# HGRN and retention rounds of a hybrid decoder layer: another order on ScalarE and DVE, and two groups of small matmuls in 64-column tiles

## The chip, the cores and the metric

The kernel runs on one core of a Trainium2 chip. The metric is the device time of one launch in microseconds (us). The kernel before takes 937.84 us, the median of 3 runs (936.68 to 938.04). TensorE, whose matmuls are called PE below, multiplies; ScalarE (ACT) and DVE read its sums from PSUM; GpSimd (POOL) works in SBUF alone; SyncE (SP) issues the weight loads.

## The reference, cut to what matters

One layer for 512 prompt rows and 8 sample rows (TT = 520 columns in the kernel, which holds everything transposed):

```
xn = rmsnorm(h); u = xn @ w_in      # hq hf hi hg (HGRN), rq rk rv rg (retention), ga gb
HGRN, 8 heads of 64:  f = lb + (1-lb)*sigmoid(hf);  S_t = diag(f_t) S_{t-1} + (1-f_t) i_t^T
                      o_t = S_t^T silu(hq_t)        # chunk by chunk for the prompt, one step for samples
retention, 4 heads of 128:  R_t = gamma R_{t-1} + k_t v_t^T,  o_t = R_t^T q_t   (rotary q, k)
a = head_rmsnorm(o) * g * silu(gate)                # for each branch
h += (sigmoid(ga)*(a_hg @ w_br_hg) + sigmoid(gb)*(a_r @ w_br_ret)) @ w_out
h += (gelu(causal_conv3(up_a)) * up_g) @ w_down;  h += sigmoid(rmsnorm(h) @ w_ple_gate) * (p @ w_ple)
y = rmsnorm(h)
```

Everything is float32.

## The kernel before

Every product with a weight matrix is done in units of 128 output rows. A unit needs `whi`, the weight rounded to the fast matmul format (made by ACT from the loaded `raw`, L832), and `wlo = raw - whi` (made by DVE, L1169, the "weight subtraction"). It is then 3 matmul pairs for each 128 rows of the inner dimension (hi by hi, hi by lo, lo by hi), 48 matmuls of 260 columns for the usual 8 chunks. There are two slots of each weight tile, by the parity of the unit. After unit k of a round, `ahead` makes the weights of unit k + 2 on ACT and on DVE.

The layer is a row of sections, each of rounds of four units: A (hq, hf), V (hi, hg), B (rq, rk, rv, rg, four rounds), C (branch gates ga and gb, four rounds), D (branch projections), E (w_out), F, G and H (feed-forward and the input embedding). The small work of the two recurrences is placed between the units:

- In round `it` of B, PE does chunk `it` of the HGRN recurrence. Seven levels of scores between halves of blocks stand in four groups, `scores(0)` to `scores(3)` (L587, L583). A level needs `zq`, the queries padded with zeros, which ACT copies from `lq` (`pad_queries`, L923), and DVE merges each level's result from the PSUM tile `lvb` into `sfull` (`merge`, L1279). `scores(1)` writes the banks that `scores(0)` wrote, so it waits for the two merges of `merge(0)`. `scores(3)` also has four matmuls by `headsel` of 2 columns (L578). POOL makes the levels' queries and keys (L1601 to L1605). After them come the outputs into `ob` (L618, L623), the mean squares of the heads (L636), and the sample outputs (L648, already in tiles of 64 columns).
- ACT then takes the square root (L971), copies the values (L974, L977), pads the first four levels of the next chunk (8 copies, L923), and after unit 3 makes `whi`, the sigmoid of rg (L983) and `ahh`, the rounded branch output (L909). DVE takes the reciprocal, the gated outputs `ot` (L1294, L1296), then after unit 3 `wlo`, `grt` (L1348), the sample column of `qT` (L1352) and `ahl = ot - ahh` (L1301). Then `merge(0)` of the next round follows.
- In round `it` of C, PE does chunk `it` of retention in the same manner: scores L659, outputs L673 and L674, mean squares L685, sample outputs L691 (8 matmuls of 128 output rows and 1 column), mean squares of the samples L698 and L699, which stand inside unit 3 after 5 of its 8 chunks. L699 releases the square root `rss` on ACT (L1006) and the sample part of the branch outputs on DVE (to L1401). D waits for the last of these.

Each engine works through its instructions in the order of the code. A wait on a semaphore holds back all that stands behind it on that engine. Queries of the first chunk are padded after the V section, and the first round of B follows at once. ACT keeps one table of functions at a time: sqrt and sigmoid lie in different ones, and an ACT_TABLE_LOAD stands wherever the next function needs the other.

Of the kernel before, what the change touches and what calls it, by code (L numbers as in the profile page):

```python
# [13 lines left out]
NS = 8  # L14
# [48 lines left out]
def hybrid_layer(nc, x_prompt, x_sample, state_hgrn, state_ret, state_conv, p_prompt, p_sample,  # L63
# [43 lines left out]
    r = Region(0, 33792)  # L107
# [136 lines left out]
    with ctx:  # L244
# [105 lines left out]
        def two(ap):  # L350
            return ap.rearrange("p (a b) -> p a b", a=2)
# [103 lines left out]
        def _(pe):  # L455
# [113 lines left out]
            def scores(use, it):  # L569


                levels = [l for l in (2 * use, 2 * use + 1) if l < LV]
                pe.wait_ge(zq_ready, it * LV + (levels[-1] + 1))
                pe.wait_ge(merged, it * MERGES + (2 * use + 1))
                taken()
                if use == 3:
                    for c in range(4):
                        pe.matmul(lvb[:, 1, 2 * c:2 + 2 * c], qk[:, c, :], headsel, start=True, stop=True)  # L578
                for l in levels:
                    for c in range(4):  # L580
                        out = lvb[:, l % 2, c * 128:(c + 1) * 128].rearrange("s (two t) -> s two t", two=2)
                        if l == LV - 1:
                            mm = pe.matmul(out[0:64], lk[l % 4][:, c, 0:64], zq[l % 4][:, c], start=True, stop=True)  # L583
                            continue
                        for r in range(2):

                            mm = pe.matmul(out[64 * r:64 * r + 64, :, 32 * r:32 * r + 32],  # L587
                                           lk[l % 4][:, c, 64 * r:64 * r + 64],
                                           zq[l % 4][:, c, :, 32 * r:32 * r + 32], start=True, stop=True)
                    mm.then_inc(sc_full, 1)  # L590
# [62 lines left out]
            with pe.Fori(0, 4) as it:  # L653
                product("C", 0, it, 0, 0, C8, 0, xah, xal)
                pe.wait_ge(staged, it * 2 + 1)
                pe.wait_ge(vst_ready, it + 5)
                wait_level(L_C, 0, it, 2)
                for h in range(4):
                    mm = pe.matmul(level(0)[:, h * 128:(h + 1) * 128], kst[:, h, :], qst[:, h, :],  # L659
                                   start=True, stop=True)  # L660
                mm.then_inc(lv_full, 1)
                wait_level(L_C, 1, it, 2)
                for h in range(4):
                    mm = pe.transpose(level(1)[:, h * 128:(h + 1) * 128], kst[:, h, :], ident)
                mm.then_inc(lv_full, 1)
                product("C", 1, it, 1, 1, C8, 0, xah, xal)
                for b in range(2):
                    pe.wait_ge(lv_free[b], it + L_C // 2 + 1)
                pe.wait_ge(o_free, it + 5)
                pe.wait_ge(staged, it * 2 + 2)  # L670
                for h in range(4):
                    out = ob[:, h * 128:(h + 1) * 128]
                    pe.matmul(out, vst[:, h * 128:(h + 1) * 128], prb[:, h, :], start=True, stop=False)  # L673
                    mm = pe.matmul(out, rst[:, h, :], qd[:, h, :], start=False, stop=True)  # L674
                mm.then_inc(ret_o, 1)
                wait_misc(M_C, 0, it, 4)
                for h in range(4):
                    mm = pe.matmul(mb[:, h * 128:(h + 1) * 128], ktk[:, h * 128:(h + 1) * 128],
                                   vst[:, h * 128:(h + 1) * 128], start=True, stop=True)
                mm.then_inc(misc_full, 1)  # L680

                product("C", 2, it, 0, 2, range(4), 0, xah, xal, last=False)
                pe.wait_ge(sq_ready, it + 5)
                wait_misc(M_C, 1, it, 4)
                pe.matmul(mb[:], ones128[:], sq[:], start=True, stop=True).then_inc(misc_full, 1)  # L685
                product("C", 2, it, 0, 2, range(4, 8), 4, xah, xal, first=False, wait_unit=False)
                wait_misc(M_C, 2, it, 4)
                pe.wait_ge(smp_staged, it + 5)
                pe.wait_ge(rsm_ready, it + 1)
                for b in range(NS):  # L690
                    mm = pe.matmul(mb[:, b:b + 1], rsm[:, b, :], qs8[:, b:b + 1], start=True, stop=True)  # L691
                mm.then_inc(misc_full, 1)

                product("C", 3, it, 1, 3, range(5), 0, xah, xal, last=False)

                pe.wait_ge(smp_sq, it + 1)
                wait_misc(M_C, 3, it, 4)
                pe.matmul(mb[:, 0:8], blk64, sqs[:, 0:8], start=True, stop=True)  # L698
                pe.matmul(mb[:, 8:16], ones128[:], sqs[:, 8:16], start=True, stop=True).then_inc(misc_full, 1)  # L699
                product("C", 3, it, 1, 3, range(5, 8), 5, xah, xal, first=False, wait_unit=False)  # L700

            pe.wait_ge(ah_lo, 17)
            with pe.Fori(0, 2) as it:
# [113 lines left out]
        def _(act):  # L817
# [16 lines left out]
            def done(sec, k, it, per=4):  # L834
                act.wait_ge(part_done, parts(sec, k, it, per) + 1)

            def ahead(sec, k, it, nxt=None):

                if k < 2:
                    hi(sec, k + 2, it)  # L840
                elif nxt is None:
                    hi(sec, k - 2, it + 1)
                else:
                    hi(nxt, k - 2, 0)
# [30 lines left out]
            for it in range(2):  # L875
                for k in range(4):
# [4 lines left out]
                    else:  # L881
                        act.wait_ge(f_done, it * 2 + (k // 2 + 1))
                        act.activation(two(sgf[:]), ps2(1), ACT.Sigmoid).then_inc(acc_free[1], 1)
            with act.Fori(0, 2) as it:
                for k in range(4):
                    done("V", k, it)
                    ahead("V", k, it)
                    if k % 2 == 0:

                        act.wait_ge(v_full, it * 4 + (k + 1))  # L890
                        act.activation(two(hiT[:]), ps2(0), ACT.Copy).then_inc(acc_free[0], 1)
                    else:
                        act.activation(two(sg[1][:]), ps2(1), ACT.Sigmoid).then_inc(sig_ready, 1)
                        act.wait_ge(v_full, it * 4 + (k + 1))
                        taken()
                        cols = bass.ds(it * 256 + 128 * (k // 2), 128)
                        act.activation(vhg[:, :, cols], m4(lvb[:, 0, :]), ACT.Copy).then_inc(v_taken, 1)
                        act.wait_ge(v_full, it * 4 + (k + 2))
                        taken()
                        act.activation(v8h[:, cols], lvb[0:NS, 1, 0:128], ACT.Copy).then_inc(v_taken, 1)  # L900

            def chunk(t, c):
                return t[:, :, bass.ds(c * CH, CH)]

# [6 lines left out]
            def pad_queries(l, it):  # L911
# [11 lines left out]
                    ins = act.activation(dst, src, ACT.Copy)  # L923
                ins.then_inc(zq_ready, 1)

            act.wait_ge(v_taken, 9)
            act.dma_start(vs_dram[0], v8h[:]).then_inc(vs_stored, 16)
            act.wait_ge(set_up, 7)
            for l in range(4):
                pad_queries(l, 0)  # L930

            def hgrn_chunk(it, last=False):
                act.wait_ge(misc_full, it * 4 + (M_B - 2))
# [35 lines left out]
                act.activation(sq[:], ob[:], ACT.Square).then_inc(sq_ready, 1)  # L969
                act.wait_ge(misc_full, it * 4 + (M_B + 3))  # L970
                act.activation(rs[:], mb[:], ACT.Sqrt, bias=eps[:]).then_inc(misc_free, 1)  # L971
                act.wait_ge(v_full, it * 2 + 10)
                taken()
                act.activation(vr[:, :, bass.ds(it * 128, 128)], m4(lvb[:, 0, :]), ACT.Copy).then_inc(v_taken, 1)  # L974
# [3 lines left out]
                if not last:  # L978
                    for l in range(4):
                        pad_queries(l, it + 1)  # L980
                done("B", 3, it)
                ahead("B", 3, it, "C" if last else None)
                act.activation(two(sg[1][:]), ps2(3), ACT.Sigmoid).then_inc(sig_ready, 1)  # L983
                branch_hi(ahh, it, 0)

            with act.Fori(0, 3) as it:
                hgrn_chunk(it)
# [165 lines left out]
        def _(dve):  # L1153
# [149 lines left out]
            with dve.Fori(0, 4) as it:  # L1303
# [40 lines left out]

                done("B", 3, it)
                ahead("B", 3, it)
                dve.wait_ge(sig_ready, it + 9)
                dve.scalar_tensor_tensor(two(grt[:, it, :]), ps2(3), vc[:, bass.ds(it + 44, 1)],  # L1348
                                         two(sg[1][:]), MUL, MUL).then_inc(acc_free[1], 1)
                dve.wait_ge(misc_full, it * 4 + (M_B + 4))  # L1350
                taken()
                dve.tensor_copy(qT[:, it, NT:TT], mb[:, 0:NS]).then_inc(misc_free, 1)  # L1352
                branch_lo(ahl, ahh, it, 0)
            step.end(4)

            dve.wait_ge(misc_free, M_C)
            with dve.Fori(0, 4) as it:
# [18 lines left out]
                dve.scalar_tensor_tensor(grown, grown, gam[:, bass.ds(it, 1)], vb[:], MUL, ADD).then_inc(rsm_ready, 1)  # L1376
                dve.wait_ge(misc_free, it * 4 + (M_C + 2))
                gate_outputs(grt, it, 4, per=3)
                done("C", 2, it)
                ahead("C", 2, it)  # L1380
                dve.wait_ge(misc_full, it * 4 + (M_C + 3))
                taken()
                dve.tensor_copy(qr[:, it, NT:TT], mb[:, 0:NS]).then_inc(misc_free, 1)
# [3 lines left out]
                cols = qT[:, it, NT:TT], qr[:, it, NT:TT]  # L1387
                dve.tensor_tensor(sqs[:, 0:8], cols[0], cols[0], MUL)
                dve.tensor_tensor(sqs[:, 8:16], cols[1], cols[1], MUL).then_inc(smp_sq, 1)
                branch_lo(arl, arh, it, 4)  # L1390
                dve.wait_ge(misc_free, it * 4 + (M_C + 4))
                step(dve.reciprocal(rss[:], rss[:]))
# [383 lines left out]
```

## Time and profile before

| what | us |
|---|---|
| median of 3 runs | 937.84 |
| the profiled execution | 936.62 |
| its span | 934.8 |
| PE busy | 911.3 (97%) |
| PE weight loads busy | 896.8 (96%) |
| DVE busy | 523.9 (56%) |
| ACT busy | 388.7 (42%) |
| POOL busy | 236.0 (25%) |

The granted clock of TensorE was 0.995 of full speed. Times in the rows are microseconds from the start of the span. V ends its last unit at about 117, B runs to about 257 and C to about 378; the rest is D to H. The time in brackets at a row's end is how long the engine sat idle before it, and who released it. A matmul's end is modelled: a following row can begin before the row above it ends, so the step from start to start is the better measure of what a group takes.

### The profile page before, as it was taken

The numbers are of one execution on the slowest core, as the hardware profiler recorded it, in microseconds if no ns is written. First come the engines' busy times: TensorE is split into PE (matmuls) and PEld (weight loads), VectorE is DVE, ScalarE is ACT, GpSimd is POOL, SyncE is SP. The second block draws the span as 40 slices with busy tenths as digits, with TensorE's granted clock in tenths as the row PEclk, the third lists the DMA queues.
The fourth block names the chain that finished last, engine by engine and source line by source line (L and its number), as shares of the span: only waits on it lengthen the run. The fifth ranks groups of instructions, "written<-read, shape, count | busy, mean of one in ns | idle before, by whom it ended". The sixth has DMA issues, their size and how long they took to land. (4 is left out here: it accounts for less than half of the span.)

```text
span 934.8 us, 20997 instructions
## 1 busy us (share of the span) xinstructions
PE 911.3 (97%) x7950; PEld 896.8 (96%) x7950; DVE 523.9 (56%) x613; ACT 388.7 (42%) x518; POOL 236.0 (25%) x289
## 2 busy tenths in 40 slices
PE   6999999999999999999999999999999999999996
PEld 5999988999999999999999999999999999999995
DVE  6432267777655655566566655555556433435653
ACT  7323356446345544323344444444443322213433
POOL 0006076777211010002631111111111021212341
PEclk9999999999999999999999999999999999999998
DMA  6333533233254434633323333333333333332212
GB/s 223 93 91 90 180 92 80 79 90 79 79 137 112 127 97 135 199 117 99 90 68 91 90 90 90 91 90 94 94 94 105 102 93 93 93 90 70 81 54 91
DMA packets 176471, 94.72 MB, mean 101 GB/s; under 512 B 17888, under 2 KB 174960, under 8 KB 176016
## 3 DMA queue, kind: packets, MB, share of 16 engines
q1 hardware_dynamic: 149698, 80.61, 29.0%
q10 hardware_dynamic: 26736, 13.60, 5.5%
q8 instruction: 25, 0.41, 0.2%
q14 instruction: 12, 0.10, 0.0%
HBM read 86.25 MB, written 8.03 MB: 101 GB/s over the span
## 5 line engine op out<-in xcount | busy, mean ns | idle before, releaser
L832 ACT ACTIVATE whi<-raw 128x1024 fp32r<-128x1024 f32 (+2 forms) x132 | 146.9, 1113 | 351.0 <-PE acc L486 350.2
L1169 DVE TENSOR_TENSOR wlo<-raw,whi 128x1024 fp32r<-128x1024 f32 (+2 forms) x132 | 195.7, 1482 | 172.3 <-ACT whi L832 172.3
L486 PE MATMUL acc<-xah,whi 128*128 128x260 f32 x896 | 186.9, 290 | 0.0
L486 PE MATMUL acc<-xah,wlo 128*128 128x260 f32 x896 | 180.2, 283 | 0.0
L486 PE MATMUL acc<-xal,whi 128*128 128x260 f32 x896 | 179.7, 282 | 0.0
L486 PE MATMUL acc<-xbh,whi 128*128 128x260 f32 x816 | 165.3, 284 | 0.8 <-issue 0.8
L486 PE MATMUL acc<-xbh,wlo 128*128 128x260 f32 x816 | 164.4, 283 | 0.0
L486 PE MATMUL acc<-xbl,whi 128*128 128x260 f32 x816 | 164.2, 283 | 0.0
L486 PEld LDWEIGHTS acc<-xah,whi 128*128 128x128 f32 x896 | 137.9, 189 | 3.3 <-issue 1.9
L486 PEld LDWEIGHTS acc<-xal,whi 128*128 128x128 f32 x896 | 137.9, 188 | 0.0
L486 PEld LDWEIGHTS acc<-xah,wlo 128*128 128x128 f32 x896 | 137.8, 188 | 0.0
L486 PEld LDWEIGHTS acc<-xbh,whi 128*128 128x128 f32 x816 | 125.8, 188 | 1.1 <-issue 1.0
L486 PEld LDWEIGHTS acc<-xbh,wlo 128*128 128x128 f32 x816 | 125.8, 188 | 0.0
L486 PEld LDWEIGHTS acc<-xbl,whi 128*128 128x128 f32 x816 | 125.5, 188 | 0.0
L486 PE MATMUL acc<-ach,whi 128*128 128x260 f32 x352 | 71.2, 283 | 0.0
L486 PE MATMUL acc<-ach,wlo 128*128 128x260 f32 x352 | 70.8, 282 | 0.0
L486 PE MATMUL acc<-acl,whi 128*128 128x260 f32 x352 | 70.6, 282 | 0.0
L1673 POOL TENSOR_TENSOR sqt<-hT 128x520 f32 x23 | 36.0, 1564 | 125.1 <-DVE hT L1426 100.8
L1693 POOL TENSOR_TENSOR gg<-gg,cv 128x520 f32<-128x520 f32 x22 | 28.9, 1313 | 118.1 <-DVE gg L1487 115.3
L486 PEld LDWEIGHTS acc<-acl,whi 128*128 128x128 f32 x352 | 54.3, 188 | 0.0
L486 PEld LDWEIGHTS acc<-ach,whi 128*128 128x128 f32 x352 | 54.1, 188 | 0.1
L486 PEld LDWEIGHTS acc<-ach,wlo 128*128 128x128 f32 x352 | 54.2, 188 | 0.0
(287 smaller groups left out, 1183.4 us busy)
## 6 DMA issues: line engine op xcount, KB each, us to landing
raw<-in_w_in SPq DMA_DIRECT2D x96, 256.0 KB, 3.1
raw<-in_w_up SPq DMA_DIRECT2D x88, 256.0 KB, 3.1
raw<-in_w_down SPq DMA_DIRECT2D x16, 384.0 KB, 3.3
raw<-in_w_down SPq DMA_DIRECT2D x16, 320.0 KB, 3.7
raw<-in_w_out SPq DMA_DIRECT2D x16, 256.0 KB, 3.0
raw<-in_w_ple_gate SPq DMA_DIRECT2D x8, 512.0 KB, 3.8
x_transposed<-xstg SPq DMA_DIRECT2D x1, 2080.0 KB, 7.5
hT<-x_transposed ACTq DMA_DIRECT2D x1, 2080.0 KB, 7.9
```

Of the source, the lines that this page charges most:

```text
L486: mm = pe.matmul(sums[:, b, 0:HT], wt[slot][:, w], xx[:, c, b * HT:(b + 1) * HT], start=first and i == 0 and q == 0, stop=last and i == n ...
L832: act.activation(whi[k % 2][:, 0:n], raw[k % 2][:, 0:n], ACT.Copy).then_inc(hi_ready, 1)
L1169: dve.tensor_tensor(wlo[k % 2][:, 0:n], raw[k % 2][:, 0:n], whi[k % 2][:, 0:n].bitcast(fp), SUB).then_inc(lo_ready, 1)
L1673: step(pool.tensor_tensor(sqt[:], hT[:, j, :], hT[:, j, :], MUL))
L1693: pool.tensor_tensor(gg[:], gg[:], cv[:], MUL).then_inc(act_ready, 1)
```

## The change

It touches sections V, B and C:

1. The first chunk's four padded query levels are made inside the second round of V, two after unit 0 and two after unit 1, not behind the section. The V loop on ACT is written out for this.
2. In each HGRN round, ACT takes a sigmoid of one column right after the square root, so that the table is loaded there.
3. In each HGRN round, `ahh` is rounded before the end of unit 3 is waited for, ahead of `whi` and the sigmoid of rg; `ahl` follows `wlo` on DVE, ahead of `grt` and `qT`.
4. In each retention round, DVE does `wlo` for the next round behind the sample sums, not ahead of them, and PE does L698 and L699 after 3 chunks of unit 3, not after 5.
5. The matmuls by `headsel` (L578) and the retention's sample outputs (L691) are split into two tiles of 64 columns each, 8 and 16 matmuls a round for 4 and 8.

```diff
@@ PE, scores() @@
                 if use == 3:
                     for c in range(4):
-                        pe.matmul(lvb[:, 1, 2 * c:2 + 2 * c], qk[:, c, :], headsel, start=True, stop=True)
+                        for r in range(2):
+                            rows = slice(64 * r, 64 * r + 64)
+                            pe.matmul(lvb[rows, 1, 2 * c:2 + 2 * c], qk[:, c, rows], headsel, start=True, stop=True)
@@ PE, section C @@
                 for b in range(NS):
-                    mm = pe.matmul(mb[:, b:b + 1], rsm[:, b, :], qs8[:, b:b + 1], start=True, stop=True)
+                    for r in range(2):
+                        rows = slice(64 * r, 64 * r + 64)
+                        mm = pe.matmul(mb[rows, b:b + 1], rsm[:, b, rows], qs8[:, b:b + 1], start=True, stop=True)
                 mm.then_inc(misc_full, 1)
-                product("C", 3, it, 1, 3, range(5), 0, xah, xal, last=False)
+                product("C", 3, it, 1, 3, range(3), 0, xah, xal, last=False)
...
-                product("C", 3, it, 1, 3, range(5, 8), 5, xah, xal, first=False, wait_unit=False)
+                product("C", 3, it, 1, 3, range(3, 8), 3, xah, xal, first=False, wait_unit=False)
@@ ACT, section V: the loop of before, written out, and in it @@
+            for it in range(2):
+                for k in range(4):
...
+                    if it == 1 and k < 2:
+
+                        act.wait_ge(set_up, 7)
+                        for l in (2 * k, 2 * k + 1):
+                            pad_queries(l, 0)
@@ ACT, ahead of section B @@
             act.wait_ge(v_taken, 9)
             act.dma_start(vs_dram[0], v8h[:]).then_inc(vs_stored, 16)
-            act.wait_ge(set_up, 7)
-            for l in range(4):
-                pad_queries(l, 0)
@@ ACT, hgrn_chunk() @@
                 act.activation(rs[:], mb[:], ACT.Sqrt, bias=eps[:]).then_inc(misc_free, 1)
+                act.activation(ssx[:, 5:6], eps[:], ACT.Sigmoid)
...
                 if not last:
                     for l in range(4):
                         pad_queries(l, it + 1)
+                branch_hi(ahh, it, 0)
                 done("B", 3, it)
                 ahead("B", 3, it, "C" if last else None)
                 act.activation(two(sg[1][:]), ps2(3), ACT.Sigmoid).then_inc(sig_ready, 1)
-                branch_hi(ahh, it, 0)
@@ DVE, section B @@
                 done("B", 3, it)
                 ahead("B", 3, it)
+                branch_lo(ahl, ahh, it, 0)
                 dve.wait_ge(sig_ready, it + 9)
...
                 dve.tensor_copy(qT[:, it, NT:TT], mb[:, 0:NS]).then_inc(misc_free, 1)
-                branch_lo(ahl, ahh, it, 0)
@@ DVE, section C @@
                 gate_outputs(grt, it, 4, per=3)
-                done("C", 2, it)
-                ahead("C", 2, it)
                 dve.wait_ge(misc_full, it * 4 + (M_C + 3))
...
                 dve.tensor_tensor(sqs[:, 8:16], cols[1], cols[1], MUL).then_inc(smp_sq, 1)
+                done("C", 2, it)
+                ahead("C", 2, it)
                 branch_lo(arl, arh, it, 4)
```

On ACT, at the end of an HGRN round, the program before has this order (`rs` is the square root, `zq` the padded queries of the next chunk, `sg` the sigmoid of rg):

```order
L971 ACT_TABLE_LOAD
L971 ACTIVATE rs<-mb,eps 128x512
...
L977 ACTIVATE v8r<-lvb 8x128
...
L923 ACTIVATE zq_122<-lq_72 64x4x64 x2
L835 REGISTER_ALU
L832 ACTIVATE whi_52<-raw_50 128x1024
L983 ACT_TABLE_LOAD
L983 ACTIVATE sg_110<-acc 128x520
L909 REGISTER_ALU
L909 ACTIVATE ahh<-ot 128x4x128
```

The changed program has, at the same place:

```order
L977 ACT_TABLE_LOAD
L977 ACTIVATE rs<-mb,eps 128x512
L978 ACT_TABLE_LOAD
L978 ACTIVATE ssx<-eps 128x1
...
L984 ACTIVATE v8r<-lvb 8x128
...
L909 ACTIVATE zq_122<-lq_72 64x4x64 x2
L895 REGISTER_ALU
L895 ACTIVATE ahh<-ot 128x4x128
L839 REGISTER_ALU
L836 ACTIVATE whi_52<-raw_50 128x1024
L991 ACTIVATE sg_110<-acc 128x520
```

The table load and `ahh` moved from behind `whi` to ahead of it.

On DVE, at the end of the same round, the program before has:

```order
L1296 TENSOR_TENSOR ot<-ot,ghg 128x512
L1167 REGISTER_ALU
L1169 TENSOR_TENSOR wlo_54<-raw_50,whi_52 128x1024
L1347 REGISTER_ALU
L1348 ISA
L1348 SCALAR_TENSOR_TENSOR grt<-acc,vc,sg_110 128x520
L1350 REGISTER_ALU
L1352 REGISTER_ALU
L1352 COPY qT<-mb 128x8
L1301 ISA
L1301 TENSOR_TENSOR ahl<-ot,ahh 128x4x128
```

And the changed one:

```order
L1303 TENSOR_TENSOR ot<-ot,ghg 128x512
L1174 REGISTER_ALU
L1176 TENSOR_TENSOR wlo_54<-raw_50,whi_52 128x1024
L1308 ISA
L1308 TENSOR_TENSOR ahl<-ot,ahh 128x4x128
L1355 REGISTER_ALU
L1356 ISA
L1356 SCALAR_TENSOR_TENSOR grt<-acc,vc,sg_110 128x520
L1358 REGISTER_ALU
L1360 REGISTER_ALU
L1360 COPY qT<-mb 128x8
```

`ahl` moved from the end to the place behind `wlo`; `grt` and `qT` are behind it now, and `merge(0)` of the next round follows them all.

On ACT, in the second round of V, the changed program has the padded queries between the units' work, where before they stood behind the whole section:

```order
L836 ACTIVATE whi_51<-raw_49 128x1024
L919 ACTIVATE hiT<-acc 128x520
L909 ACTIVATE zq_119<-lq_69 64x4x64 x2
L909 ACTIVATE zq_120<-lq_70 64x4x64 x2
L836 ACTIVATE whi_52<-raw_50 128x1024
L921 ACTIVATE sg_110<-acc 128x520
L925 ACTIVATE vhg<-lvb 128x4x128
L928 ACTIVATE v8h<-lvb 8x128
L909 ACTIVATE zq_121<-lq_71 64x4x64 x2
L909 ACTIVATE zq_122<-lq_72 64x4x64 x2
L836 ACTIVATE whi_51<-raw_49 128x1024
```

The eight copies stand behind units 0 and 1 of the second round.

## Rows read from the trace of the kernel before

**Rows 1.** Waits of PE, whole span: total us, times, longest.

```profile
PE lvb L587 <- DVE sfull L1279: 2.1, 3, 0.8
PE lvb L587 <- ACT zq L923: 1.8, 2, 1.6
```

**Rows 2.** Timeline of ACT in V: start, us, instruction, idle before.

```profile
101.90 1.06 ACT L832 ACTIVATE whi<-raw 128x1024 fp32r<-128x1024 f32 x1 [4.13 <-PE acc L486]
...
116.90 2.20 ACT L923 ACTIVATE zq<-lq 64x256 f32<-64x256 f32 x5 [0.76 <-ACT v8h L900]
```

**Rows 3.** Timeline of ACT at the end of the first HGRN round.

```profile
146.59 0.69 ACT L971 ACTIVATE rs<-mb,eps 128x512 f32<-128x512 f32 x1 [2.77 <-PE mb L636]
...
151.36 1.06 ACT L832 ACTIVATE whi<-raw 128x1024 fp32r<-128x1024 f32 x1
152.44 1.28 ACT L983 ACT_TABLE_LOAD   x1
...
153.73 0.61 ACT L983 ACTIVATE sg<-acc 128x520 f32<-128x520 f32 x1
154.23 0.62 ACT L909 ACTIVATE ahh<-ot 128x512 f32 x1
```

**Rows 4.** Timeline of DVE over the same stretch.

```profile
151.54 0.69 DVE L1296 TENSOR_TENSOR ot<-ot,ghg 128x512 f32<-128x512 f32 x1
152.45 1.23 DVE L1169 TENSOR_TENSOR wlo<-raw,whi 128x1024 fp32r<-128x1024 f32 x1 [0.22 <-ACT whi L832]
154.52 0.76 DVE L1348 SCALAR_TENSOR_TENSOR grt<-acc,vc,sg 128x520 f32 x1 [0.84 <-ACT sg L983]
...
155.27 0.89 DVE L1301 TENSOR_TENSOR ahl<-ot,ahh 128x512 f32 x1
156.08 1.32 DVE L1279 COPY_PREDICATED sfull<-msk,lvb 128x512 f32<-128x512 uint32 x1
157.56 1.31 DVE L1279 COPY_PREDICATED sfull<-msk,lvb 128x512 f32<-128x512 uint32 x1 [0.15 <-DVE sfull L1279]
```

**Rows 5.** Timeline of PE at scores(1) of the second round.

```profile
159.02 1.15 PE L587 MATMUL lvb<-zq,lk 128*64 128x64 f32 x32 [0.78 <-DVE sfull L1279]
```

**Rows 6.** Timelines of DVE, POOL and PE where B gives way to C.

```profile
257.88 0.69 DVE L1296 TENSOR_TENSOR ot<-ot,ghg 128x512 f32<-128x512 f32 x1
...
260.29 0.16 DVE L1352 COPY qT<-mb 128x8 f32 x1
260.71 0.81 POOL L1662 COPY qst<-qr 128x512 f32 x1 [5.83 <-DVE qT L1352]
263.13 1.05 PE L659 MATMUL lvb<-qst,kst 128*128 128x128 f32 x8
```

**Rows 7.** Timeline of PE: small groups of one round of B and C.

```profile
131.59 0.95 PE L578 MATMUL lvb<-cst,qk 128*128 128x2 f32 x8
149.90 1.10 PE L648 MATMUL mb<-qz,ss 128*64 128x1 f32 x32
279.49 1.84 PE L691 MATMUL mb<-qs,rsm 128*128 128x1 f32 x16
284.87 0.28 PE L698 MATMUL mb<-sqs,cst 128*128 128x8 f32 x2
```

**Rows 8.** Waits of PE's weight loads: total us, times, longest.

```profile
PEld mb L636 <- DVE sbd L1339: 1.0, 3, 0.4
```

**Rows 9.** Timeline of DVE in the first round of C.

```profile
282.46 1.22 DVE L1169 TENSOR_TENSOR wlo<-raw,whi 128x1024 fp32r<-128x1024 f32 x1
...
284.06 0.16 DVE L1389 TENSOR_TENSOR sqs<-qr 128x8 f32 x1
```

**Rows 10.** Timelines of ACT and PE at the end of C.

```profile
373.67 1.28 ACT L1006 ACT_TABLE_LOAD   x1
375.69 0.28 ACT L1006 ACTIVATE rss<-mb,eps 128x16 f32<-128x16 f32 x1 [0.74 <-PE mb L699]
...
378.50 0.51 PE L486 MATMUL acc<-ahh,whi 128*128 128x260 f32 x2 [0.60 <-DVE arl L1401]
```

More of the change, by code:

```diff
@@ L883, in _ @@
                         act.activation(two(sgf[:]), ps2(1), ACT.Sigmoid).then_inc(acc_free[1], 1)
[L884 to L900, printed above, removed]
             def chunk(t, c):
@@ L924, in pad_queries @@
                 ins.then_inc(zq_ready, 1)
+            for it in range(2):
+                for k in range(4):
+                    done("V", k, it)
+                    ahead("V", k, it)
+                    if k % 2 == 0:
+                        act.wait_ge(v_full, it * 4 + (k + 1))
+                        act.activation(two(hiT[:]), ps2(0), ACT.Copy).then_inc(acc_free[0], 1)
+                    else:
+                        act.activation(two(sg[1][:]), ps2(1), ACT.Sigmoid).then_inc(sig_ready, 1)
+                        act.wait_ge(v_full, it * 4 + (k + 1))
+                        taken()
+                        cols = slice(it * 256 + 128 * (k // 2), it * 256 + 128 * (k // 2) + 128)
+                        act.activation(vhg[:, :, cols], m4(lvb[:, 0, :]), ACT.Copy).then_inc(v_taken, 1)
+                        act.wait_ge(v_full, it * 4 + (k + 2))
+                        taken()
+                        act.activation(v8h[:, cols], lvb[0:NS, 1, 0:128], ACT.Copy).then_inc(v_taken, 1)
+                    if it == 1 and k < 2:
+                        act.wait_ge(set_up, 7)
+                        for l in (2 * k, 2 * k + 1):
+                            pad_queries(l, 0)
             act.wait_ge(v_taken, 9)
             act.dma_start(vs_dram[0], v8h[:]).then_inc(vs_stored, 16)
-            act.wait_ge(set_up, 7)
-            for l in range(4):
-                pad_queries(l, 0)
             def hgrn_chunk(it, last=False):
```

## The prediction, written before the changed kernel was run

> **What bounds the kernel now.** I read the busy shares first: PE is busy for 911.3 of 934.8 us, so time is made or lost only where PE stands still or does slower work. The list of PE's waits gives the places: 2.1 us in three waits of scores (L587) for DVE's merges and 1.8 us in two for the padded queries on ACT, the longest 1.6 [rows 1]. A fourth is 0.60 us at the start of section D [rows 10]. The timelines around these show which chain of ACT and DVE ends last. PE's weight loads also show 1.0 us in three small waits for the HGRN state on DVE [rows 8]. All else of the change lies beside PE, and counts only if its delay reaches one of these places or makes a new one.
>
> **1. Padded queries inside V.** The wait of 1.6 us is the one at the first scores: ACT starts the eight copies only at 116.90, behind `v8h`, which ended 0.76 earlier at 116.14 [rows 2]. Inside V the copies take four times 0.44 us (five took 2.20) after each of two units, where ACT otherwise sits idle for 4.13 us ahead of the next `whi` [rows 2]; that idle time hides them. What is late next is `v8h` itself, at 116.14, about 1 us before PE arrives. Without that cover the old 1.6 us would return. Gain: -1.6. The second, short wait for ACT stays, because its chain starts at the end of unit 0 and moves with PE.
>
> **2. The end of an HGRN round, three times.** Here the change delays DVE. ACT is busy without a break from the square root to `ahh`: `whi` starts at 151.36 as soon as the padded queries are through, not when PE is ready [rows 3]. Moved ahead of it are now the table load, 1.28; the one-column sigmoid, about 0.2; and `ahh`, which takes a place of 0.5 (0.62 long, with some overlap: the step from `sg` at 153.73 to `ahh` at 154.23). `ahh` itself does not wait, since `ot` ends at 152.23 [rows 4] and ACT gets there only at 151.36 + 1.48 = 152.84. So `whi` ends at 152.42 + 1.98 = 154.4 instead of 152.42.
>
> DVE then does `wlo`, `ahl`, `grt`, `qT` and `merge(0)`. From start to start `wlo` takes 1.15 and the other three together 1.56 (154.52 to 156.08) [rows 4]. New start of the merges: 154.43 + 1.15 + 1.56 = 157.14, before 156.08, so 1.06 later. The 0.84 us that DVE idled for the sigmoid [rows 4] is filled, but the late `whi` costs more than that. `wlo` now meets POOL's next level, which it did not before; `ahl`, at the place where POOL works, took 0.89 where the like-sized `ot` took 0.69 [rows 4]. For that I add 0.1 and take +1.15. Bounds: 0.8 (`ahl` back to 0.69 and the one-column sigmoid free) and 1.7 (`wlo` and `grt` stretched by the same 0.89/0.69, 0.37 and 0.2).
>
> No slack swallows this: the merges end at 158.87, and PE starts scores(1) at 159.02 after 0.78 idle for them [rows 4, 5]. Behind these scores on PE stands everything else, so it is paid in full in all three rounds that have a next one: 3 x 1.15 = +3.45.
>
> On ACT's switch of tables, the row shows 1.28 us, with 0.02 before it and 0.01 behind it [rows 3]. The Trainium skill ("ScalarE: Activation LUTs", What ACT_TABLE_LOAD costs) gives 1.283 us for the load and 1.38 us of drain besides. By that rule each of the three rounds would be 1.4 us worse; the trace agrees with the load and shows no drain.
>
> **3. From B to C.** In the last HGRN round no queries are padded, and ACT waits for PE with `whi`. Now `ahh` stands ahead of it and waits for `ot`, which ends at 258.57 [rows 6]. From there: `ahh` at 258.8, `whi` from 259.3 to 260.35, `wlo` at 260.38, `ahl` at 261.53, `grt` at 262.14, `qT` from 262.8 to 262.97; before, it ended at 260.45. That copy releases `qst` on POOL, 0.26 later and 0.81 long [rows 6], so it ends at 264.05, and PE, which started L659 at 263.13 without a wait [rows 6], starts it at 264.1. Cost: +0.95; its bounds are 0.6 (uncontended `qst`, 0.2 less, and 0.15 of wake-up) and 1.3.
>
> **4. The group by headsel.** L578 goes from 8 recorded matmuls of 128 columns, 0.95 us, to 16 of 64. The nearest row is L648, which has 32 of 64 columns in 1.10 [rows 7], so 16 are 0.55; with 0.1 for the change of tile width the gain is 0.3 a round. In rounds 0 to 2 it is lost: L636 already waits for DVE [rows 8], whose chain starts at the end of unit 1, before this group, and PE would only wait longer. The last round has no such wait: -0.3.
>
> **5. The retention's sample outputs and sums.** L691 has 16 records in 1.84; 32 like those of L648 take 1.10 [rows 7]. Allowing 0.2 for two changes of width, I take 0.55 as the gain in the group (bounds 0.4 and 0.74). On PE, L698 was at 284.87 [rows 7]; it would come 0.55 earlier, and another 1.44 earlier for 12 matmuls of 0.12 that now stand behind it: 282.88. DVE must have `sqs` ready: the `qr` copy now starts where `wlo` did, 282.46. Before, it started as `wlo` ended (283.68, less 0.08 of overlap), and `sqs` ended at 284.22 [rows 9], 0.62 later; so now at 283.1, and PE at 283.15. A new wait of 0.25 follows, behind which PE's two sums and the rest of unit 3 stand. Net -0.3 in each of rounds 0 to 2: -0.85 in all. `wlo`, 0.6 later, is hidden by the 30 matmuls of unit 3, 3.6 us, that PE still does before it uses it.
>
> In round 3 the chain to D decides. `rss` waited until 375.69 for L699; now the sum is there at 374, and the table load ends at 374.95 [rows 10]. So `rss` and all behind it comes 0.7 earlier, and with it PE's start of D at 378.50. PE itself could be 1 us earlier, so the gain is the chain's: -0.7.
>
> **The sum.** -1.6 + 3.45 + 0.95 - 0.3 - 0.85 - 0.7 = +0.95. The profiled execution took 936.62 (span 934.8), 1.2 below the median of 937.84, so I add the sum to each: 937.6 for a profile, 938.8 for the median. By the ends of the bounds it is from -0.6 to +3.1. A change within 0.2%, 1.88 us, can't be told from none.
>
> **Rivals.**
>
> Faster: the end of the round does not move. That is so if ACT's table load fits in time in which it would wait anyway. For it: ACT idles 2.77 us ahead of `rs` [rows 3]. Against it: the new load stands behind `rs`, where ACT goes on without a break until `ahh`. The time would be -1.6 - 0.3 - 0.85 - 0.7 = -3.45 (the entry to C then costs nothing either): 934.4.
>
> Slower: the two DVE instructions that now meet POOL's work stretch. The place is `wlo` and `ahl` between two HGRN rounds, and it decides from 1.46 a round on (0.95 + 3 x 0.31 = 1.88). For it: `ahl` at 0.89. At 1.8 a round, the sum is 0.95 + 3 x 0.65 = +2.9: 940.7.
>
> Narrow tiles don't pay. If each of the small matmuls kept its 0.11 us (1.84 over 16), L691 would take 3.5 and L578 1.8, and PE would lose 1.7 and 0.85 a round, 4 x 2.55 = +10 against the gains of parts 4 and 5: about 949. Against it stands L648 at 0.034 each [rows 7]. The Trainium skill ("TensorEngine Tiling (Array Packing)", Instruction Overhead) says that a matmul of one column has the latency of one with 60, and under Key Properties that a change of mode drains the engine; by that rule more and narrower matmuls gain nothing. The trace of L648 disagrees as to the count.
>
> The change gives nothing either way: the first wait only passes to the release of the value bank, and the rest cancels: 937.5 to 938.3.
>
> **Chances.** Forecast 0.55, faster rival 0.14, slower rival 0.22, narrow tiles 0.03, nothing 0.06. The first and the last lie within 0.2%, less a tail of 0.01 to slower and 0.02 to faster, and about a tenth of the slower rival falls short of the bound: same 0.60, faster 0.16, slower 0.24. The range of the forecast alone is 937.2 to 940.9; with half of the faster rival and the contended case taken in it is 935.6 to 941.3.
>
> **What would show it.** Part 1: no wait for `zq` at the first scores. Part 2: `whi` at the round's end starts about 2 us later after the square root, and the wait of L587 for merges grows from 0.8 to about 1.9 each. Part 3: a new wait of PE L659 for POOL's `qst`, near 1 us. Part 4: L578 near 0.6 us, with the wait at L636 near 0.5. Part 5: L691 near 1.1, a wait of 0.25 at L698, and D's wait gone or under 0.2. The prediction is wrong if the merges' wait stays at 0.8, or if C starts without a wait.

## The result, and the profile after

The changed kernel takes 940.96 us, the median of 7 runs (939.98 to 942.49), against 937.84: 1.0038 times as long, with a 95% interval of 1.0028 to 1.0048. It is slower. The forecast of 938.8 and "no change to be told" was wrong; the time lies in the range of 935.6 to 941.3.

The page after, its first parts, with the granted clock (PEclk) by fortieths of the span:

```profile
span 939.0 us, 21162 instructions
...
PE 912.9 (97%) x8046; PEld 896.8 (96%) x8046; DVE 523.4 (56%) x613; ACT 388.4 (41%) x522; POOL 239.0 (25%) x289
...
PEclk9999999999999999999999999999999999999998
```

Nothing there tells the loss; the waits of PE do. The same view as [rows 1], for the changed kernel (`sfull` from DVE is what the merges write):

```profile
PE lvb L589 <- DVE sfull L1286: 5.5, 3, 1.9
PE mb L638 <- DVE sbd L1346: 1.1, 3, 0.4
PE mb L702 <- DVE sqs L1394: 0.8, 4, 0.2
PE lvb L661 <- POOL qst L1669: 0.7, 1, 0.7
PE lvb L589 <- ACT zq L909: 0.3, 1, 0.3
```

The wait for queries at the first scores is gone, the three waits for merges have grown from 2.1 to 5.5, and there are new ones at L702 and L661. Why the merges are late stands in the timelines of ACT and DVE at the end of the first HGRN round, which answer to [rows 3] and [rows 4]:

```profile
146.00 0.69 ACT L977 ACTIVATE rs<-mb,eps 128x512 f32<-128x512 f32 x1 [2.76 <-PE mb L638]
146.71 1.28 ACT L978 ACT_TABLE_LOAD   x1
148.01 0.20 ACT L978 ACTIVATE ssx<-eps 128x1 f32<-128x1 f32 x1
...
148.75 3.50 ACT L909 ACTIVATE zq<-lq 64x256 f32<-64x256 f32 x8
152.28 0.64 ACT L895 ACTIVATE ahh<-ot 128x512 f32 x1
152.81 1.04 ACT L836 ACTIVATE whi<-raw 128x1024 fp32r<-128x1024 f32 x1
...
153.76 0.58 ACT L991 ACTIVATE sg<-acc 128x520 f32<-128x520 f32 x1
```

```profile
150.96 0.69 DVE L1303 TENSOR_TENSOR ot<-ot,ghg 128x512 f32<-128x512 f32 x1
153.89 1.23 DVE L1176 TENSOR_TENSOR wlo<-raw,whi 128x1024 fp32r<-128x1024 f32 x1 [2.24 <-ACT whi L836]
155.03 0.89 DVE L1308 TENSOR_TENSOR ahl<-ot,ahh 128x512 f32 x1
155.84 0.75 DVE L1356 SCALAR_TENSOR_TENSOR grt<-acc,vc,sg 128x520 f32 x1
...
156.58 1.30 DVE L1286 COPY_PREDICATED sfull<-msk,lvb 128x512 f32<-128x512 uint32 x1
158.04 1.31 DVE L1286 COPY_PREDICATED sfull<-msk,lvb 128x512 f32<-128x512 uint32 x1 [0.15 <-DVE sfull L1286]
```

From the start of the square root to the start of `whi` it is 6.81 us, against 4.77 in [rows 3]. DVE now idles 2.24 us for `whi`, where it idled 0.22 + 0.84 in [rows 4], and the merges start 10.58 after the square root did, not 9.49. The timeline of PE in the third HGRN round of the changed kernel shows the wait, and something behind it that was not forecast:

```profile
196.18 1.15 PE L589 MATMUL lvb<-zq,lk 128*64 128x64 f32 x32 [1.85 <-DVE sfull L1286]
197.26 0.77 PE L486 MATMUL acc<-xah,whi 128*128 128x260 f32 x2
197.82 0.64 PE L486 MATMUL acc<-xal,whi 128*128 128x260 f32 x2
198.25 0.64 PE L486 MATMUL acc<-xah,wlo 128*128 128x260 f32 x2
```

Pairs of matmuls of 260 columns follow each other in 0.43 us there, where it is 0.24 elsewhere. The stretch view says why. Its columns are: stretch, us, busy of PE, PEld, DVE, ACT and POOL, each with its count, then the granted clock:

```profile
190.00:197.20 7.20, 5.35 (x90) 4.99 (x88) 5.41 (x7) 4.22 (x8) 5.58 (x11) 1.00 0.47 124
197.40:200.70 3.30, 3.30 (x16) 3.30 (x17) 3.15 (x5) 1.46 (x4) 3.06 (x7) 0.50 0.16 36
201.00:207.00 6.00, 6.00 (x85) 5.66 (x85) 2.43 (x4) 1.00 (x2) 3.68 (x7) 1.00 0.29 87
```

The granted clock is 0.50, the lower of its two levels (1.2 GHz), for 3.4 us, beginning 1.1 us behind the end of the wait. The product between this group of scores and the next (24 records) takes 4.60 us from start to start in place of 3.07: 1.53 lost. Before, the clock stands at 1.00 in the same place. The start and the end of that product, in the kernel before and then the end in the changed one:

```profile
195.78 0.51 PE L486 MATMUL acc<-xah,whi 128*128 128x260 f32 x2
198.85 1.15 PE L587 MATMUL lvb<-zq,lk 128*64 128x64 f32 x32
201.86 1.15 PE L589 MATMUL lvb<-zq,lk 128*64 128x64 f32 x32
```

The accounts from start to start of the same groups in the two profiles, in us, after minus before (C is the section with the retention rounds, D the branch projections):

| place | forecast | measured |
|---|---|---|
| start-up of the program, ahead of the change | 0 | +1.07 |
| first scores, queries in V | -1.6 | -1.62 |
| three waits for merges | +3.45 | +3.33 |
| half clock behind one of them | - | +1.53 |
| headsel group, last round | -0.3 | -0.21 |
| entry to C | +0.95 | +0.85 |
| three retention rounds | -0.85 | -0.24 |
| end of C | -0.7 | -0.72 |
| section D | 0 | +0.19 |
| sum (the spans, 934.8 and 939.0, differ by 4.13) | +0.95 | +4.18 |

The first line is no effect of the change. In the changed profile the clock is at its lower level for 3.4 us from 16.4 us on, ahead of all that the change moves. Such a stretch, beginning at 15.1 to 17.9 us, is in the profiles of all eleven experiments, some of which leave everything ahead of section B as it was; the profile shown of before lacks it, and only that. The 45 runs of the kernel before that were taken beside the experiments lie at 936.1 to 939.9, without a gap near 937; that the shortest of them are the ones without the stretch is an inference, since none of them has a profile.

### The profile page after: what moved, and what is told of

Its sections match the earlier page's. It is cut to its first block and busy times, and to the rows that moved or that the text cites. A ratio compares the mean times of both kernels' runs of the same rounds, so it can differ in the third digit from the quotient of the medians.

```text
span 939.0 us, 21162 instructions
## 1 busy us (share of the span) xinstructions
PE 912.9 (97%) x8046; PEld 896.8 (96%) x8046; DVE 523.4 (56%) x613; ACT 388.4 (41%) x522; POOL 239.0 (25%) x289
```

## Experiments

The time in brackets is the kernel before on the same chip. Parts are numbered as in the list of the change.

**Undoing the order at the end of the HGRN round.** All else of the change kept:

```diff
-                act.activation(ssx[:, 5:6], eps[:], ACT.Sigmoid)
...
-                branch_hi(ahh, it, 0)
                 done("B", 3, it)
...
+                branch_hi(ahh, it, 0)
@@ DVE @@
-                branch_lo(ahl, ahh, it, 0)
                 dve.wait_ge(sig_ready, it + 9)
...
+                branch_lo(ahl, ahh, it, 0)
```

> The changed kernel with the end of the HGRN round as it was (no early table load, ahh and ahl at their old places: parts 2 and 3 of the change undone), all else kept. Theory, that this order alone costs: the wait of scores(1) for the merges back at 0.8 a round, no wait at L661, no drop of TensorE's clock between the start and the end, and a time of 937.8 - 1.6 - 0.2 - 0.8 = about 935.2. Rival, that the loss is in the retention rounds or the narrow tiles: the time stays at 938 or above.

Measured: 935.30 (937.52), ratio 0.9973 (0.9963 to 0.9984), faster than before. The waits of PE:

```profile
PE lvb L589 <- DVE sfull L1285: 2.0, 3, 0.8
```

and none at L661. So the loss lies in this order; the rest of the change gains 2.2 us.

**That order alone**, the reverse edit on the kernel before:

```diff
+                act.activation(ssx[:, 5:6], eps[:], ACT.Sigmoid)
...
+                branch_hi(ahh, it, 0)
                 done("B", 3, it)
...
+                branch_lo(ahl, ahh, it, 0)
                 dve.wait_ge(sig_ready, it + 9)
```

> The kernel before with only the new end of the HGRN round (parts 2 and 3). Theory: three waits of 1.9 us for merges in place of 0.8 (+3.3), a wait at L659 of about 0.9, and, in at least one round, a stretch of half clock behind the long wait (+1.5): about 943. Rival, that the half clock was chance or came from another part: 942.0 or less, and no such stretch in the records.

Measured: 942.38 (937.52), ratio 1.0050 (1.0036 to 1.0064).

```profile
PE lvb L587 <- DVE sfull L1280: 5.4, 3, 1.8
PE lvb L587 <- ACT zq L923: 1.8, 2, 1.6
PE lvb L659 <- POOL qst L1663: 0.7, 1, 0.7
```

The waits are as expected, and the profile has a half-clock stretch at 236.3, 1.4 us behind the end of the third of them; in the changed kernel it was behind the second. The profiled execution took 944.62; three of the five runs took 941.95 to 942.38, which is little more than the waits alone (+4.2, 941.7). It is likely that these three had no such stretch, but they have no profile.

**Part 2 alone (early table load).**

```diff
                 act.activation(rs[:], mb[:], ACT.Sqrt, bias=eps[:]).then_inc(misc_free, 1)
+                act.activation(ssx[:, 5:6], eps[:], ACT.Sigmoid)
```

> The kernel before with part 2 alone: the one-column sigmoid behind the square root in each HGRN round. Theory: whi comes 1.4 later, the sigmoid of rg at about its old time, and the merges 0.5 later a round; C is entered without a wait, since ACT waits for PE there: +1.5, about 939.1, and no half clock behind waits of 1.3. Rival, that the early load is hidden: no change, 937.6.

Measured: 940.41 (938.23), ratio 1.0026 (1.0017 to 1.0035), 11 runs: +2.2 for an expected +1.5. The merges come 0.77 later a round, not 0.5: `ahl`, still last, took 1.10, where it took 0.89 in [rows 4]. C is entered without a wait, and there is no half clock behind the waits of up to 1.6, as expected.

```profile
157.07 1.10 DVE L1302 TENSOR_TENSOR ahl<-ot,ahh 128x512 f32 x1
```

**Part 3 alone (ahh and ahl earlier).**

```diff
+                branch_hi(ahh, it, 0)
                 done("B", 3, it)
                 ahead("B", 3, it, "C" if last else None)
                 act.activation(two(sg[1][:]), ps2(3), ACT.Sigmoid).then_inc(sig_ready, 1)
-                branch_hi(ahh, it, 0)
@@ DVE @@
+                branch_lo(ahl, ahh, it, 0)
                 dve.wait_ge(sig_ready, it + 9)
...
-                branch_lo(ahl, ahh, it, 0)
```

> The kernel before with part 3 alone: ahh ahead of whi on ACT, ahl ahead of grt on DVE, the table load where it was. Theory: whi is only 0.5 late, DVE fills its wait for the sigmoid with ahl, the merges come 0.3 earlier a round (-0.9), and the entry to C costs 1.3: +0.4, about 938.0. Rival, that any late whi costs its delay: 3 x 0.5 + 1.3 = +2.8, 940.4.

Measured: 942.36 (938.23), ratio 1.0041 (1.0027 to 1.0054). The expected 938.0 was wrong, and the rival's 940.4 too low. The timeline of ACT there:

```profile
153.23 0.63 ACT L909 ACTIVATE ahh<-ot 128x512 f32 x1 [1.10 <-DVE ot L1296]
153.76 1.04 ACT L832 ACTIVATE whi<-raw 128x1024 fp32r<-128x1024 f32 x1
154.82 1.28 ACT L984 ACT_TABLE_LOAD   x1
```

Without the early table load ACT reaches `ahh` before `ot` exists and waits 1.10 us for DVE, with `whi` behind it. So `whi` is 1.6 late and not 0.5, the merges 0.92 late, and the entry to C costs 1.3. The two parts are not additive: 0.77 and 0.92 alone, 1.06 together, since the table load fills the time in which ACT would have waited for `ot`.

**A needless delay in place of the change.** One DVE instruction ahead of the merges, on the kernel before:

```diff
                 branch_lo(ahl, ahh, it, 0)
+                step(dve.reciprocal(rs[:, 0:170], rs[:, 0:170]))
```

> The kernel before with nothing moved, and one needless DVE reciprocal of 170 columns (about 1.1 us) at the end of each HGRN round, ahead of the merges; its result is not used. Theory, that only the lateness of DVE's merges matters, and that the long standstill of TensorE brings the half clock: waits of about 1.9 us as in the changed kernel, +3.3 for them, and a half-clock stretch, +1.5: about 942.6. Rival, that the clock has to do with the other edits: +3.3 and no half clock: 941.1.

Measured: 946.09 (937.52), ratio 1.0076 (1.0062 to 1.0090). The instruction and its own semaphore cost 1.8 a round, not 1.1, so the waits were 2.6 and not 1.9; the test was too strong. Its profile has two half-clock stretches, the first 1.5 us behind the end of such a wait, the second 0.1 us behind the end of another:

```profile
PE lvb L587 <- DVE sfull L1279: 7.7, 3, 2.6
```

```profile
163.80:167.20 3.40, 3.40 (x18) 3.40 (x17) 3.25 (x5) 0.85 (x3) 3.16 (x6) 0.50 0.02 4
201.30:204.70 3.40, 3.40 (x39) 3.28 (x39) 2.07 (x3) 1.43 (x4) 2.28 (x5) 0.50 0.24 56
```

I therefore ran it with 64 columns, which makes the merges as late as the change does, and with 8.

```diff
+                step(dve.reciprocal(rs[:, 0:64], rs[:, 0:64]))
```

> As e3_dve_delay, with 64 columns in place of 170, which should make the merges 1.1 later a round, as the change does. Theory, that lateness of the merges and the half clock behind long waits are all: 3.3 for the waits, and half-clock stretches as in the changed kernel: +4 to +5, about 942.5. Rival, that the half clock needs the other edits: +3.3, 941.3, at the granted clock of the kernel before.

Measured: 941.99 (937.57), ratio 1.0044 (1.0028 to 1.0060). The waits are nearly those of the changed kernel (1.94, 1.92 and 1.67 for 1.84, 1.85 and 1.80), and its profile has no half clock behind any:

```profile
PE lvb L587 <- DVE sfull L1279: 5.5, 3, 1.9
```

Of its six runs three took 940.02 to 940.83, at a mean clock of 0.994 to 0.996, and three 943.14 to 943.25, at 0.991; the median lies in the gap between the two groups. The profiled one, 940.83, fits the waits alone (+3.3). That the three slower ones had half clock behind a wait is not shown, since they have no profile. Nothing of the change is in this kernel but the late merges.

```diff
+                step(dve.reciprocal(rs[:, 0:8], rs[:, 0:8]))
```

> The same with 8 columns: the merges come about 0.75 later a round. Theory, that the half clock comes only with the longest waits: +2.2 and no more, about 940.2, and a mean granted clock as before. Rival, that any longer wait brings it at times: over +3, 941.2, with a lower clock in some runs.

Measured: 939.90 (937.57), ratio 1.0024 (1.0014 to 1.0034), waits up to 1.6. Ten of twelve runs are 938.26 to 940.70; two are 941.51 and 941.99, at a clock of 0.992. Its profile, at 940.70, has no half clock behind a wait. Whether the two slow runs had some is not shown: of the 45 runs of the kernel before, whose waits are 0.8, two are as slow and lower still in clock (939.34 and 939.93, at 0.990).

**The changed kernel again.** No edit.

> The changed kernel as it is, run again beside the kernel before on the same chip. Theory: +1.6 from waits and small matmuls, and one half-clock stretch of 1.5 in nearly every run, seen as a mean granted clock lower by 0.002: +3.1, about 941. Rival, that the stretch in its profile was a single event: +1.6, about 939.5, at an equal clock.

Measured: 940.92 (937.57), ratio 1.0038 (1.0024 to 1.0052). Its profiled execution took 939.44, the shortest of the six, with a span of 937.7 and no half clock between 19 and 926 us; the other five took 940.07 to 943.43. The half clock in the middle of the first profile is thus not in every execution.

This span is 2.83 longer than the 934.83 of before. Only 0.05 of that is the start-up: it has the half-clock stretch, but PE was 1.1 us ahead when it began. The places that the change touches give 1.65, where the account of the first profile without its half clock gives 4.18 - 1.07 - 1.53 = 1.58. The remaining 1.13 lies in the last 13 us, where all kernels are the same. The granted clock falls to 0.50 at 926.5, and the last matmuls of the program still stand behind that; before, it fell at 926.3, just as they ended. First the group before the last, in the kernel before and here, then the stretch view here:

```profile
924.56 1.27 PE L804 MATMUL mb<-ones,tg 128*128 128x1 f32 x10 [0.80 <-DVE tg L1540]
926.26 1.90 PE L808 MATMUL mb<-ones,tg 128*128 128x1 f32 x10 [0.79 <-DVE tg L1547]
926.60:937.60 11.00, 2.64 (x14) 2.21 (x13) 3.77 (x12) 3.21 (x8) 0.00 (x0) 0.50 0.50 194
```

The mean granted clock does not tell the two places apart: it is 0.992 in both profiles of the changed kernel, the one with half clock in the middle and the one without. So neither the time nor the mean clock of an unprofiled run shows where its clock was low.

**Part 4 of the change undone too**, on the kernel of the first experiment: sums after 5 chunks, `wlo` ahead of the sample sums.

```diff
-                product("C", 3, it, 1, 3, range(3), 0, xah, xal, last=False)
+                product("C", 3, it, 1, 3, range(5), 0, xah, xal, last=False)
...
-                product("C", 3, it, 1, 3, range(3, 8), 3, xah, xal, first=False, wait_unit=False)
+                product("C", 3, it, 1, 3, range(5, 8), 5, xah, xal, first=False, wait_unit=False)
@@ DVE @@
+                done("C", 2, it)
+                ahead("C", 2, it)
                 dve.wait_ge(misc_full, it * 4 + (M_C + 3))
...
-                done("C", 2, it)
-                ahead("C", 2, it)
```

> The kernel of e1_no_hgrn_order with part 4 undone too: sums after 5 chunks, wlo ahead of the sample sums; the narrow tiles and the padded queries in V stay. Theory: L698 comes just as DVE has the sums ready, so the 0.55 that the narrow tiles save in L691 is kept in all four rounds, where part 4 kept 0.1 in three and 0.5 in the last: 1.3 faster than e1, about 934.0. Rival, that part 4 is a gain of its own: slower than e1, 935.8 or more.

Measured: 934.38 (938.23), ratio 0.9960 (0.9947 to 0.9974), against 0.9973 with part 4: better by 1.2 us, as expected, though the two intervals overlap (the spans of the two profiles also differ by 1.2). The 0.8 us of waits at L702 are gone from its profile, and D's wait of 0.6 for `arl` is back.

**A better order: merges first.** On DVE, on the kernel of the first experiment:

```diff
                 dve.tensor_copy(qT[:, it, NT:TT], mb[:, 0:NS]).then_inc(misc_free, 1)
+                if not last:
+                    merge(0, it + 1)
                 branch_lo(ahl, ahh, it, 0)
```

> The kernel of e1_no_hgrn_order, and on DVE the merges of scores(0) of the next round stand ahead of ahl, so that ahl (0.9 us) is out of the chain that scores(1) waits for. Theory: the three merge waits of 0.8 go to nearly nothing, the short wait for zq at scores(2) of 0.3 appears in each round in their place: -1.5 against e1, about 933.7. Rival, that something else is as late as the merges: 935.2 as e1.

Measured: 933.64 (937.52), ratio 0.9961 (0.9947 to 0.9975). Three of the five runs took 932.87 to 933.64, at a mean clock of 0.994, and two 935.45 and 935.78, at 0.992; so such slower runs come without long waits for merges too. No wait for merges is left:

```profile
PE mb L638 <- DVE sbd L1343: 1.1, 3, 0.4
PE mb L702 <- DVE sqs L1399: 0.8, 4, 0.2
PE lvb L589 <- ACT zq L909: 0.7, 3, 0.3
```

**And three more waits taken out:**

```diff
+                pad_queries(4, it)
                 for k, scale in ((0, 1.0), (1, KSCALE)):
...
-                        for l in range(4, LV):
+                        for l in range(5, LV):
@@ DVE: state growth ahead of wlo of unit 2 @@
-                done("B", 2, it)
-                ahead("B", 2, it)
                 dve.wait_ge(o_ready, it + 1)
...
                 grown.then_inc(misc_free, 1)
+                done("B", 2, it)
+                ahead("B", 2, it)
@@ PE @@
-                product("C", 3, it, 1, 3, range(3), 0, xah, xal, last=False)
+                product("C", 3, it, 1, 3, range(4), 0, xah, xal, last=False)
```

> The kernel of e4_merges_first with three more edits: level 4 of the padded queries is made before the end of unit 0 is waited for (scores(2) then need not wait 0.3 for ACT, four rounds), DVE grows the HGRN state ahead of wlo of unit 2 (L638 then need not wait 0.3 to 0.6, three rounds), and the sample sums stand after 4 chunks, not 3 (no wait at L702, 0.35 in three rounds). Theory, that each wait is gone and no other chain ends right behind it: -1.2 - 1.2 - 1.1, about 930.2. Rival, that other chains are nearly as late: a third of that, 932.5.

Measured: 929.76 (938.23), ratio 0.9909 (0.9894 to 0.9924), four runs from 929.51 to 930.09. It beats both kernels. In sections V to D one wait of PE is left:

```profile
PE acc L486 <- DVE arl L1413: 0.4, 1, 0.4
```

## Why the prediction was wrong, step by step

The parts are numbered here as in the prediction: 4 is the group by headsel, 5 the retention's sample outputs and sums.

**Parts 1 to 3 held.** The first wait went (-1.62 for -1.6). The merges were 1.05, 1.01 and 1.27 late for 1.15; `whi` was late by the table load, the short sigmoid and `ahh`, which was the whole of the step. The entry to C cost 0.85 for 0.95, with the wait at L661 for `qst`, which took 0.61 there and not 0.81. The table load itself was 1.28 us, with 0.02 before it and 0.02 behind; the drain of 1.38 us that the Trainium skill ("ScalarE: Activation LUTs", What ACT_TABLE_LOAD costs) adds did not show here either, though ACT was busy up to it.

**Part 4 held**: the group by headsel took 0.49 from start to start where it had taken 0.88, and in the first three rounds PE stood longer at L638 instead (1.1 us in three waits); 0.21 came out in the last.

**Part 5 was mis-sized**, the term "net -0.3 in each of rounds 0 to 2": it measured -0.11, 29.98 us a round for 30.09, and once, in the first round, the group behind the wait for `qst` took 0.1 back, so that the three rounds came to -0.24 for -0.85. L695 saved more than taken, 0.67 from start to start, and the wait for `sqs` was there:

```profile
284.62 1.10 PE L695 MATMUL mb<-qs,rsm 128*64 128x1 f32 x32
288.25 0.38 PE L702 MATMUL mb<-sqs,cst 128*128 128x8 f32 x2 [0.19 <-DVE sqs L1394]
```

But the wait and what goes with it cost 0.37, the tile change ahead of L695 0.09, and L702 behind the wait took 0.24 from start to start, not 0.14. Where the prediction had a gain of 0.55 less a wait of 0.25, it was 0.58 less 0.47. The step "narrow tiles pay" was right, and the rival against it fell. Without the earlier sums (part 4 of the change) the saving is worth more, as the experiment on them shows. The end of C gave what was forecast (-0.72 for -0.7).

**The step that failed is the sum's premise**, that a wait of PE costs its own length: "3 x 1.15 = +3.45" has no term for the clock. The size of the waits was right (+3.33), and the clock was put at nothing without a reason. In the first profile 1.53 us was lost to half clock behind one of the waits. The rest of the account is +1.58 for +0.95, nearly all of the difference in part 5; that alone would have given 939.4, still no change to be told. With 1.5 for the clock as well, it is 940.9, and the measured median is 940.96.

For the medians this is an inference. They rose by 3.1, and by 3.4 in the second set, so 1.5 to 1.8 more than the account. The second profile has no half clock behind a wait, and loses 1.13 to half clock at its end. How often each of the two occurs in the runs without a profile, and how often in those of the kernel before, is not known.

That late merges can bring half clock without any edit of the change is shown by the needless delay, with two stretches behind waits of 2.6. At the length of the changed kernel's waits the matched delay shows the cost of the waits, but its profile has no such stretch. In all thirteen profiles there are four stretches of half clock between the start-up and the last 13 us, and each begins 0.1 to 1.5 us behind the end of a wait of 1.8 us or more for merges. Behind ten other waits of that length there is none, two of them 1.92 and 1.94 long and one 2.56. Why it comes behind one such wait and not behind the next, equal one stays open.

The faster rival fell: no idle time of ACT stood behind the square root. The slower rival had its sign right, but not its mechanism: the stretch of `wlo` and `ahl` under POOL's work was absent (1.23 and 0.89). That its 940.7 lies next to the measured time is luck.

## What to carry to other kernels

Before moving work ahead on a helper engine, look whether its predecessor there waits for anything: a load or a copy is hidden only in time in which the engine would stand, and behind a busy chain it delays all that follows. If the chain ends in a standstill of TensorE, count the standstill and what its clock may do after it. Ask which instruction is the one that another engine waits for, and put that first: one reordered pair here, the merges ahead of `ahl`, gave 1.7 us by the medians, where the early table load and the early `ahh` together had cost 4.9.

## What was not expected of the hardware

- Behind standstills of PE of 1.8 us and more, between stretches of dense matmuls, the granted clock fell to 0.50 for 3.4 us in some cases: behind one of three waits in the profiles of the changed kernel and of the order alone, two of three at 2.6 us, none of three in the matched delay and in the changed kernel's second profile. The one worked out above cost 1.5 us.
- The same fall stands at 15 to 18 us, in the start-up, in 12 of the 13 profiles taken, all but the one shown of before. In the two profiles of the changed kernel PE lost 1.2 and 1.1 us there.
- At the end of the program the clock fell to 0.50 in all 13 profiles. In seven of them it did so as the last matmuls ended or later, and the stretch from the start of the last-but-one `ob` group (L776, L780 in the changed kernel) to the end took 12.75 to 12.78 us; in the other six it fell earlier, and the stretch took 13.09 to 13.90. So up to 1.1 us of this program's time hung on that alone, whatever was changed.
- 32 recorded matmuls of one column in alternate 64-column tiles took 1.03 us, 16 of 128 columns with the same data 1.70.
